# One-hot blocks moved between three engines in a fused attention and PEER kernel: GpSimd makes tile 2's unweighted blocks, ScalarE takes three of VectorE's groups of tile 1

## The reference, cut to what matters

```
s1, i1 = top_k(s[:, :, 0], 16); s2, i2 = top_k(s[:, :, 1], 16)      # 128 keys on each side
cand_s = s1[..., :, None] + s2[..., None, :]; cand_i = i1 * 128 + i2
top_s, pos = top_k(cand_s, 16); experts = take_along_axis(cand_i, pos)
g = softmax(top_s)
a = gelu(einsum("td,thkd->thk", xc, u_tab[ec]))                     # 128 dots per token
out = einsum("thk,thkd->td", g * a, v_tab[ec])                      # 128 weighted rows per token
```

## Time and profile before

| | us |
|---|---|
| median of 3 runs | 2037.63 |
| lowest and highest run | 2035.4, 2044.22 |
| the profiled execution, its own time | 2045.1 |
| its span, first to last instruction | 2043.8 |
| busy in the span: PE, DVE, ACT, POOL | 1800.4, 1497.3, 925.4, 630.8 |

### The profile page before, as it was taken

The page is one execution under the profiler, slowest core; times in us unless marked ns, Lnnn a source line. Parts: engine busy times, 40 slices in busy tenths (PEclk is TensorE's granted clock), DMA queues, the critical chain, the costliest instruction groups (busy, mean ns, idle before and its releaser), DMA issues.

```text
span 2043.8 us, 28687 instructions
## 1 busy us (share of the span) xinstructions
PE 1800.4 (88%) x11068; PEld 1601.6 (78%) x11068; DVE 1497.3 (73%) x1987; ACT 925.4 (45%) x1474; POOL 630.8 (31%) x549
## 2 busy tenths in 40 slices
PE   6999999999999999957765353699999999999997
PEld 6999999999999887746764243578878888888886
DVE  4464444444465548988889899878878889998997
ACT  5444444444444441223433999644333343343433
POOL 0000000001044003477777677112211114454430
PEclk9999999999999999978998555899999999999999
DMA  9555555555466869999999999498999999999994
GB/s 310 167 170 168 166 167 174 174 165 167 144 185 219 316 242 419 364 402 410 410 406 412 372 409 396 165 346 343 396 387 374 398 376 375 396 404 399 403 400 193
DMA packets 293543, 627.88 MB, mean 307 GB/s; under 512 B 10364, under 2 KB 223405, under 8 KB 234958
## 3 DMA queue, kind: packets, MB, share of 16 engines
q0 software_dynamic: 48400, 343.95, 41.8%
q1 hardware_dynamic: 244558, 282.20, 40.4%
q10 hardware_dynamic: 496, 0.58, 0.1%
HBM read 622.45 MB, written 8.44 MB: 309 GB/s over the span
## 4 chain that ended last, share of the span: by engine, by line
PE 72%; DVE 9%; ACT 8%; DMA 5%; POOL 3%; DVEq 2%; issue 1%; SPq 0%; ACTq 0%; POOLq 0%
PE ps L2010 34%; PE ps L1671 27%; DVE u_ring L1494 4%; PE ps L1838 4%; PE ps L1852 3%; DMA u_ring<-in_peer_u,idx_all 3%; DVEq L1444 2%; ACT ones L1131 2%; ACT ones L1140 1%; ACT ones L1137 1%; POOL u_ring L707 1%; ACT u_ring L1072 1%; POOL u_ring L698 1%; DMA raw<-in_w_out 1%; DMA v_raw<-in_peer_v 1%
## 5 line engine op out<-in xcount | busy, mean ns | idle before, releaser
L1253 DVE TENSOR_TENSOR w_lo<-raw,w_hi 128x2048 fp32r<-128x2048 f32 x112 | 259.0, 2313 | 324.5 <-ACT w_hi L780 324.5
L1671 PE MATMUL ps<-act_hi,w_hi 128*128 128x256 f32 x1536 | 442.1, 288 | 4.6 <-DVE act_lo L1377 2.9
L1671 PE MATMUL ps<-act_lo,w_hi 128*128 128x256 f32 x1536 | 435.9, 284 | 0.0
L1671 PE MATMUL ps<-act_hi,w_lo 128*128 128x256 f32 x1536 | 435.8, 284 | 0.0
L1188 ACT ACTIVATE v_hi<-v_raw 128x2048 fp32r<-128x2048 f32 x128 | 245.5, 1918 | 405.7 <-PE ps L2010 205.8
L2010 PE MATMUL ps<-v_hi,c_hi 128*128 128x512 f32 x1024 | 403.9, 394 | 4.3 <-DVE c_lo L1569 4.3
L2010 PE MATMUL ps<-v_hi,c_lo 128*128 128x512 f32 x1024 | 403.6, 394 | 0.0
L2010 PE MATMUL ps<-v_lo,c_hi 128*128 128x512 f32 x1024 | 402.6, 393 | 0.0
L1565 DVE TENSOR_TENSOR v_lo<-v_raw,v_hi 128x2048 fp32r<-128x2048 f32 x128 | 293.2, 2291 | 73.9 <-ACT v_hi L1188 73.4
L1494 DVE CUSTOM_DVE_ANT_0 u_ring<-u_ring,ps 128x2048 f32<-128x2048 f32 x144 | 326.3, 2277 | 23.0 <-DMA u_ring<-in_peer_u,idx_all 22.6
L780 ACT ACTIVATE w_hi<-raw 128x2048 fp32r<-128x2048 f32 x112 | 214.1, 1911 | 262.8 <-PE ps L1671 217.5
(11 more groups left out here) (246 smaller groups left out, 2258.9 us busy)
## 6 DMA issues: line engine op xcount, KB each, us to landing
v_raw<-in_peer_v SPq DMA_DIRECT2D x128, 1024.0 KB, 7.3
raw<-in_w_in SPq DMA_DIRECT2D x80, 1024.0 KB
raw<-in_w_out SPq DMA_DIRECT2D x16, 1024.0 KB
wq<-in_peer_w_q SPq DMA_DIRECT2D x8, 2048.0 KB, 13.8
raw<-in_w_br_a SPq DMA_DIRECT2D x16, 512.0 KB
bias_by_query<-bias_by_distance POOLq DMA_DIRECT2D x1, 4096.0 KB, 21.2
bias_st<-bias_by_query POOLq DMA_DIRECT2D x16, 256.0 KB, 4.5
raw<-in_w_br_b SPq DMA_DIRECT2D x16, 256.0 KB
```

The source lines that it names most:

```text
L1253: nc.vector.tensor_tensor(w_lo[:, j % NHL], raw[:, j % NRAW], w_hi[:, j % NHL].bitcast(F32), ALU.subtract).then_inc(lo_done, 1)
L1671: last = nc.tensor.matmul(out_ap, w_parts[wp][:, slot, k], act_parts[ap][:, k], start=(k == k0 and m == 0), stop=(k == k1 - 1 and m == 2))
```

## The change

- GpSimd makes the unweighted blocks of tile 2's twelve groups: four compare instructions for each (`tensor_scalar` with `is_equal` on 128x128, no Abs and Relu), in front of the gathers with the numbers `KEYS_AT` in `EARLY`: 156, 158, 161, 164, 166, 169, 172, 174, 177, 180, 182 and 185, that is from (9, 12) to (11, 9). Before the first it waits for `kt_ev`. ScalarE's `key_ones` goes, with its semaphore `ka_ok`.
- ScalarE makes 24 of tile 1's groups and not 21, VectorE 8 and not 11. ScalarE's stand at 7, 6, 6 and 5 places of units 8 to 11 (before: 7, 7, 6, 1); VectorE's at 3, 3 and 2 places of units 9 to 11 (before: 4, 4, 3). Its last place is (11, 8), where it was (11, 9).

```diff
-ACT_GROUP_AT = {at: n for n, at in enumerate([(8, k) for k in (3, 4, 6, 8, 10, 12, 14)] + [(9, k) for k in (0, 2, 4, 7, 9, 11, 14)]
-                                             + [(10, k) for k in (0, 3, 5, 8, 11, 13)] + [(11, 1)])}
-DVE_GROUP_AT = {at: n for n, at in enumerate([(9, k) for k in (1, 5, 9, 14)] + [(10, k) for k in (1, 5, 9, 14)] + [(11, k) for k in (1, 5, 9)])}
+ACT_GROUP_AT = {at: n for n, at in enumerate([(8, k) for k in (3, 4, 6, 8, 10, 12, 14)] + [(9, k) for k in (1, 4, 6, 9, 11, 14)]
+                                             + [(10, k) for k in (0, 3, 5, 8, 11, 13)] + [(11, k) for k in (0, 3, 5, 8, 11)])}
+DVE_GROUP_AT = {at: n for n, at in enumerate([(9, k) for k in (3, 8, 13)] + [(10, k) for k in (3, 8, 13)] + [(11, k) for k in (3, 8)])}
+KEYS_AT = {156 + 8 * g // 3: g for g in range(N_PRE)}
...
+        def key_ones(g):
+
+            if g == 0:
+                pool.wait_ge(kt_ev, 1)
+            for m in range(GTOK):
+                last = nc.gpsimd.tensor_scalar(pre[g // 4][:, g % 4, m], iota_f[:, :], pick2[:, 1, GTOK * g + m:GTOK * g + m + 1], None, ALU.is_equal)
+            last.then_inc(pre_ok, 1)
...
+            if n in KEYS_AT:
+                key_ones(KEYS_AT[n])
             if k == 0:
                 pool.wait_ge(idx_ok, u + 1)
...
-        def key_ones(g):
-
-            rows = pre[g // 4][:, g % 4]
-            for m in range(GTOK):
-                last = nc.scalar.activation(rows[:, m], iota_f[:, :], ACT.Abs, scale=-1.0, bias=pick2[:, 1, GTOK * g + m:GTOK * g + m + 1])
-            last.then_inc(ka_ok, 1)
-            act.wait_ge(ka_ok, g + 1)
-            nc.scalar.activation(rows, rows, ACT.Relu, scale=-1.0, bias=one_col[:, :]).then_inc(pre_ok, 1)
...
-            if c == N_EARLY - 1 and 2 <= k < 2 + N_PRE:
-                key_ones(k - 2)
```

More of the change, by code:

```diff
@@ L454, in build @@
     kt_ev = sem("kt_ev")
-    ka_ok = sem("ka_ok")
     pre_ok = sem("pre_ok")
```

## The result

The changed kernel takes 2055.56 us in the median of 7 runs (2051.01 to 2063.71) against 2038.73 for the kernel before in as many (2035.4 to 2044.22). The ratio is 1.0084, 95% interval 1.0063 to 1.0104: slower by 0.84%, some 17 us, where I had forecast 5.4 us of gain, 2032.2, and a range from 2026 to 2043. The profiled execution took 2058.4 us, its span is 2057.1 us, 13.3 us longer than before.

What follows compares the result with a forecast made beforehand. From 1180 to 1270 us ScalarE, VectorE and DMA were nearly full; after the change GpSimd's chain would bind the last dot. 4.2 us there plus 1.2 us idle time gave 5.4 us: 2037.6 to 2032.2, range 2026 to 2043.

Steps and rivals of the forecast that it cites:

- the price of a compare: GpSimd's 128x128 compare with a column operand: taken as 0.35 us, range 0.28 to 0.45; twelve blocks 15.6 us.
- GpSimd's waits hide the blocks: Between the gathers of (9, 12) and (11, 9), 13.5 us of GpSimd waits were to cover the twelve blocks.
- GpSimd's compares are dear: Rival, chance 0.14: each 0.1 us more per compare adds 4.8 us to GpSimd's chain; above about 0.52 the change loses.
- waits that vanish: The 2.5 us of GpSimd waits left before the gather of (11, 9), subtracted when dearer compares use them up.
- My sum for GpSimd's chain: Gather of (11, 9) at 1257.5, last gather 1272.5, row landed 1280.0, dot done 1282.3: 4.2 us earlier.
- The square of the last dots: ScalarE's squaring after VectorE's last dot would no longer be late; 1.2 of 1.7 us idle time counted as gain.
- its own 8.9 us: ScalarE's net saving: 23.0 us of key blocks and 1.4 of copies out, 15.5 of three groups in.
- the 1279 that I had: Forecast start of ScalarE's `high_v(0)`: 1277.2 from less work, 1279 with 2 us for waits on late products; before 1286.14.
- Late groups, clock: After the early dots, late groups, clock and v loop stay unchanged: same instructions, all hung on the last coefficients.
- VectorE's term: Three one-hot groups less on VectorE: last dot 2.0 to 5.2 us earlier by its own work, 4.5 taken.
- the port: Rival, chance 0.13: VectorE's groups and coefficients wait so often for GpSimd that the saving is eaten; 2 us slower, 2039.6.
- DMA's bound of 5.9 us: In the 90 us stretch, transfers at full rate need 84.1 us, so DMA allows at most 5.9 us of gain.

Runs made afterwards that it cites:

- late keys and new places: Changed kernel with all twelve key blocks behind the last early gather and VectorE's eight groups at picks 1, 6 and 11: 0.9986 of the kernel before.
- run with late keys: Changed kernel with all twelve key blocks moved behind the last early gather, groups still at picks 3, 8 and 13: 1.0032 of the kernel before.
- split version: Changed kernel, groups at 1, 6, 11; five key blocks before gathers, three behind the last early gather, four after the last coefficients: 0.9967 of the kernel before.

## Why the prediction was wrong

**The step that failed is the price of a compare**, 0.35 us in my sum and 0.616 measured: 12.8 us on GpSimd's chain, and with it the claim that GpSimd's waits hide the blocks. The rival "GpSimd's compares are dear" had the mechanism and the direction, but I had given it 0.14 and set 0.45 as the end that the two 128-column rows allow. They do not: neither is an instruction with an operand that is a column. For something that no row shows, rows of other kinds are no upper bound, and the own length of the queue (73.1 us, of which 59.6 work) said that 13.5 us of cover carry twelve blocks of at most 1.1 us, 0.28 a compare. Most of the price range lay beyond that.

The price was the largest error, but not the only one. By the rival's own sum 0.616 us gives 12.8 - 2.5 us of waits that vanish, less 0.5 us more of idle time gained: 4.4 us slower than before, 2042.0, still inside my range. For the profiled execution that is 2049.5, and it took 2058.4. The other 9 us are other terms of the sum, listed below: the landing of the last row 3.9, the square 2.2, the start of the stretch 1.9, the late groups 0.9, the waits 0.7.

My sum for GpSimd's chain against the profile after, term by term (us):

| | forecast | measured | off by |
|---|---|---|---|
| gather of (9, 12), behind the first block | 1181.1 | 1182.99 | +1.9 |
| from there to the gather of (11, 9) at 1270.36 | 76.4 | 87.37 | +11.0 |
| to the last gather, 1285.14 | 15.0 | 14.8 | -0.2 |
| to the end of the last dot, 1298.8 | 9.8 | 13.7 | +3.9 |

- *11.0.* Eleven of the twelve blocks lie in this stretch. 44 compares at the mean of 0.616 are 27.1 us, and GpSimd's busy time rose by just that, 80.69 - 53.58. I had 14.3 for them: +12.8. Of waits and issue I had left 2.5 + 6.0 = 8.5, and 87.37 - 80.69 = 6.7 remained: -1.8. The term was mis-sized by its price.
- *1.9.* In the changed profile all work before the stretch ran 1.7 us earlier, so it is really 3.6: 2.9 by the 3.08 us wait behind the group at (9, 3), and 0.7 by the first block, dearer than I had it.
- *3.9.* I had let the last row land 7.5 us after its issue, since the queue of transfers would be short. The last seven gathers took 7.5, 8.9 and 11.6 us (shortest, median, longest) to land: GpSimd issued them at 2.5 us each once the blocks were over, about as fast as they are moved, and the queue filled again.
- *The square of the last dots.* Forecast: VectorE's idle time falls from 1.88 to 0.7. It was 2.38. ScalarE's loop did become shorter in work, but it waited 20.7 us for products, so `high_v(0)` started at 1298.95, after the last dot. It hung on GpSimd, not on its own 8.9 us. With GpSimd out of the way (late keys and new places) it started at 1277.51, near the 1279 that I had. Just ahead of it stands, in both, a wait of 2.17 us that I had not counted: ScalarE's last group, at (11, 11), is now the end of its loop, and it waits for TensorE's product of it.
- *Late groups, clock.* Forecast as unchanged; from their start to the v loop 22.06 us before and 23.00 after. The granted clock is a bit lower over that stretch, 0.87 against 0.93: it was at full from about 4 us behind their start before, from about 7 after.

Together 16.6 + 1.7 + 0.9 over 2039.7 is 2058.9; the profiled execution took 2058.4.

**VectorE's term came out, but by luck.** In the changed kernel the eight groups took 23.1 us (busy us, mean ns):

```profile
L1523 DVE TENSOR_SCALAR ones_d<-iota_f,pickT 128x128 f32<-128x128 f32 x32 | 12.4, 468 | 0.0
L1529 DVE TENSOR_TENSOR ones_d<-iota_f,pickT 128x512 f32<-128x512 f32 x8 | 10.7, 1332 | 0.0
```

That is 6.2 us less than the 29.3 of eleven groups, where I had 4.5, and 2.9 a group, so the port did not decide. It is worth nothing under 22.0 us of waiting for rows. And it holds only because GpSimd was late there. My view was that a stall stands at a place which the new table leaves. The run with late keys shows that the new places take 37.3 us for eight groups, where the mean of before would give 21. GpSimd starts the two halves of the products beside the dots of k = 3, 4, 8, 9, 13, 14, and the new groups stand right behind 3, 8 and 13: the code said so, and I read collisions as chance with a mean. With GpSimd out of the way, this is worth 0.46% (1.0032 against 0.9986).

**What was right.** The port: VectorE's one-hots do wait for GpSimd's products and compares. The Trainium skill's rule (page "SBUF — State Buffer", section "Who interferes with whom") of an exclusive lock held for a whole instruction agrees with this. The small instruction, which had two SBUF inputs, fits it at 0.60 and 0.67 us, which is a wait of no more than one compare of 0.59 us. At 4.33 us it sat through several compares, which the rule alone does not say. ScalarE's busy time fell from 925.4 to 917.4 us, 8.0 for the 8.9 counted. DMA's bound of 5.9 us for the stretch is where the run with late keys and new places stands, at 424 GB/s. And a gain of this size was there to be had, 6.7 us in the split version.

What stays open: why a VectorE instruction sometimes waits for several GpSimd instructions in a row and sometimes for one (4.33 us against 0.60 and 0.67); no run separates them. The upstream part of the profiles also differs by up to 6.6 us from run to run (VectorE's write of `idx_all` ahead of the stretch starts between 1159.0 and 1165.6 us), so single profiles are compared here by their stretches and not by their ends.

## What to carry to other kernels

Before work goes to an engine that issues gathers, add up that engine's queue over the stretch, issue included: its waits there are all the cover that the new work has, and the price at which they are full is worth more than a guess at the price. An engine at 31% of the span was at 82% in the stretch that mattered, issue included. Where two engines block each other's port, place by what the other engine is made to start at that pick, since the collision is then the rule and not chance, as long as that engine keeps up: once GpSimd was late, places 1, 6 and 11 were no better than 3, 8 and 13.

## What the hardware showed that was not expected

- A GpSimd compare of 128x128 with a column operand takes 0.59 us, of 128x512 1.58 us; a memset of 128x128 0.22.
- A 16-column VectorE instruction with two SBUF inputs took 4.33 us beside GpSimd compares in an unbroken row in one run, 0.60 and 0.67 in two others, and 0.18 us with a gap there.
- With 330 GB/s moved, the share of busy DMA time was still 0.90: the share does not say how far from the full rate (424 to 427 GB/s) the transfers are.
